# Squares of the RMS norms: VectorE adds the first five or four tiles, TensorE sums that tile and the rest

## The chip, the core and the metric

The kernel runs on one NeuronCore of a Trainium2 chip. The metric is device time in microseconds of one launch, the median over several runs. The engines meant below are TensorE (PE in the profile, PEld for its weight loads), VectorE (DVE), ScalarE (ACT), GpSimd (POOL) and SyncE (SP), whose queue starts most of the weight transfers.

## The reference, cut to what matters

A residual stream `x` of 256 tokens by 1024 features passes through ten sublayers, each of which begins with an RMS norm of `x`:

```python
def rms_norm(h, gain):
    h32 = h.astype(jnp.float32)
    h32 = h32 * lax.rsqrt(jnp.mean(h32 * h32, axis=-1, keepdims=True) + EPS)
    return (h32 * gain.astype(jnp.float32)).astype(h.dtype)

# first block, for each of 2 layers
h = rms_norm(x, norm_g[layer, 0]) * (1.0 + scale[:, :, 0]) + shift[:, :, 0]
x = x + 0.5 * gate[:, :, 0] * swiglu(h, ffn_w_in[layer, 0], ffn_w_down[layer, 0])
...   # then attention or hgrn2, whose last product is "@ w_o", then swiglu again
# second block, for each of 2 layers
x = x + sliding_window_attention(rmsnorm(x, norm_mix[i]), ...)   # or short_gated_conv
x = x + peer_ffn(rmsnorm(x, norm_ffn[i]), ...)
```

The change concerns only the sum of squares over the 1024 features, `mean(h32 * h32)`.

## The kernel before

`x` lies transposed in SBUF as `xT`: features on the 128 partitions, in KD = 8 tiles of 256 tokens. A norm needs, for each token, a sum over 8 tiles and 128 partitions. ScalarE squares a tile of `xT` into a tile of `sq` as soon as that tile has its final value, and TensorE sums over the partitions: the tile of squares is the stationary operand, a column of ones moves, and the result goes to one column of the PSUM bank `mz[:, 0]`. `sums(n, a, b)` does it for tiles a to b-1 of norm n, with two matmuls a tile (one for each half of the tokens). The sum then goes to ScalarE (square root), VectorE (reciprocal) and back to TensorE, which spreads it over the partitions (`spread_norm`).

Weights are float32 and are split in two parts. A chunk of weights lands in `raw` (four slots), ScalarE copies its high part to `w_hi` (L1534), VectorE subtracts and writes the low part `w_lo` over `raw` (L2108), and TensorE multiplies with both. `lo_ready` tells TensorE that a chunk is split; `w_used` tells SP, ScalarE and VectorE that TensorE is done with it, and a slot is filled again only then. Each engine has one hand-written order of work, and all of it waits on counting semaphores.

Two places stand ahead of a norm, four times each.

* The second feed-forward product, `ffn` with the phase `ffn_down`, ahead of norms 1, 3, 4 and 6. It has eight pairs `rp` of two chunks `j` (11 tiles of weights each). A pair makes one tile of `xT`, which VectorE adds at its end (`add_to_x`, L2211 and L2213). TensorE calls `sums` for one tile ahead of the second chunk of pairs 2 to 6 (tiles 0 to 4), and ahead of each chunk of pair 7 (tiles 5 and 6). In each pair VectorE splits two chunks, in the first three of these phases does up to two columns of the modulation (`modulation`, L2176, on `ada_raw`, which ScalarE fetches), from pair 5 on makes two tiles of the next product's input (`raw_low`, L2133), and then waits for `w_used` and adds to `xT`.
* The output projection, `out_product`, ahead of norms 2, 5, 7 and 9. It has four chunks `c`, each of which makes two tiles of `xT`. After chunk 2 TensorE sums tiles 0 and 1, after chunk 3 tiles 2 and 3. VectorE splits, calls `raw_low` for the two tiles of the chunk before, waits for `w_used` and adds to `xT`.

Behind both, `raw_pair` starts the next phase on the not yet normalized `x` (L639 to L641), sums the remaining tiles of squares between its matmuls, and begins with

```python
pe.wait_ge(evac_done, ph.evac0)
pe.wait_ge(lo_ready, 2 * pair + 2)
```

so it waits until both chunks of its first pair are split; VectorE does that during the last chunks of the phase before. Norm 0 stands at the kernel's start: there VectorE adds all eight tiles of squares (L2925). Norm 8 stands behind the experts and is not touched.

Of the kernel before, what the change touches and what calls it, by code (L numbers as in the profile page):

```python
# [30 lines left out]
AX = mybir.AxisListType  # L31
# [37 lines left out]
def raw_pairs(ph):  # L69

    return ph.pairs if ph.kind in ("swa", "query", "conv") else RAW_PAIRS

# [144 lines left out]
def build(nc, x, cols, const, pick, lvmask, rel, bucket, c_row, ada, ffn_in, ffn_down, attn, out_w, hgrn, swa, conv,  # L217
# [10 lines left out]
    with ExitStack() as ctx:  # L228
# [189 lines left out]
        norm_sq, norm_sum, norm_rms = sem("norm_sq"), sem("norm_sum"), sem("norm_rms")  # L418
        norm_inv, norm_wide = sem("norm_inv"), sem("norm_wide")
# [171 lines left out]
        def _(pe):  # L591
# [7 lines left out]
            def sums(n, a, b):  # L599

                for k in range(a, b):
                    pe.wait_ge(norm_sq, KD * n + k + 1)
                    for tb in range(TB):
                        last = mm(mz[:, 0, tb:tb + 1], sq[:, k, tb * P:(tb + 1) * P], ones[:, 0:1], start=(k == 0 and tb == 0),
                                  stop=(k == KD - 1), skip_group_check=True)
                if b == KD:
                    last.then_inc(norm_sum, 1)
# [192 lines left out]
            def ffn(q, n):  # L800
# [10 lines left out]
                for rp, pair, half, lap in each_pair(ph):  # L811
                    if rp > 1:
                        pe.wait_ge(x_done, KD * n + rp - 1)
                    for j in range(2):
# [4 lines left out]
                        if j and 1 < rp < KD - 1:  # L819
                            sums(n + 1, rp - 2, rp - 1)  # L820
                        if rp == KD - 1:
                            sums(n + 1, rp - 2 + j, rp - 1 + j)
# [463 lines left out]
            def out_product(i, n, opening=halves_first):  # L1286
# [21 lines left out]
                for rp, pair, half, lap in each_pair(ph.part(1, ph.pairs - 1)):  # L1308
                    for j in range(2):
                        c = 2 * rp + j  # L1310
                        pe.wait_ge(lo_ready, 2 * pair + j + 1)
                        pe.wait_ge(x_done, KD * n + 2 * c - 2)
                        for t in range(2):
                            last = tile_product(pp[:, j, t], 2 * half + j, t * KD, us, 0, KD, KD - 1)
                        last.then_inc(w_used, 1)
                        sums(n + 1, 2 * c - 4, 2 * c - 2)
# [783 lines left out]
        def _(dve):  # L2100
# [107 lines left out]

            def add_to_x(ps, g, xk, done):
# [5 lines left out]
            def ffn(q, n):  # L2215
# [39 lines left out]
                for rp, pair, half, lap in each_pair(ph):  # L2255
# [3 lines left out]
                    if rp > 4:  # L2259
                        for k in range(2 * rp - 10, 2 * rp - 8):  # L2260
                            raw_low(n + 1, k)
                    if rp == 7:
# [13 lines left out]
            def out_product(i, n):  # L2276
# [3 lines left out]
                for rp, pair, half, lap in each_pair(ph):  # L2280
                    for j in range(2):
# [4 lines left out]
                        if c:  # L2286
                            raw_low(n + 1, 2 * c - 2)
                            raw_low(n + 1, 2 * c - 1)
                        dve.wait_ge(w_used, 2 * pair + j + 1)
# [919 lines left out]
```

## Time and profile before

| | us |
|---|---|
| median of 3 runs | 2913.57 (2910.48 to 2914.21) |
| the profiled execution, its own time | 2913.14 |
| its span, first to last instruction | 2911.3 |
| TensorE busy with matmuls | 2801.7 (96%) |
| VectorE busy | 2300.0 (79%) |
| ScalarE busy | 1379.6 (47%) |

The busy times count instructions of an engine that overlap in time once. The profiled execution stands within 0.5 us of the median, so a time read from its rows can be compared with the runs. "Idle before" names the time in which the engine did nothing ahead of an instruction, with what ended it.

### The profile page before, as it was taken

The numbers are of one execution on the slowest core, as the hardware profiler recorded it, in microseconds if no ns is written. First come the engines' busy times: TensorE is split into PE (matmuls) and PEld (weight loads), VectorE is DVE, ScalarE is ACT, GpSimd is POOL, SyncE is SP. The second block draws the span as 40 slices with busy tenths as digits, with TensorE's granted clock in tenths as the row PEclk, the third lists the DMA queues.
The fourth block names the chain that finished last, engine by engine and source line by source line (L and its number), as shares of the span: only waits on it lengthen the run. The fifth ranks groups of instructions, "written<-read, shape, count | busy, mean of one in ns | idle before, by whom it ended". The sixth has DMA issues, their size and how long they took to land.

```text
span 2911.3 us, 48985 instructions
## 1 busy us (share of the span) xinstructions
PE 2801.7 (96%) x19360; PEld 2600.1 (89%) x19360; DVE 2300.0 (79%) x3460; ACT 1379.6 (47%) x1553; POOL 816.1 (28%) x663
## 2 busy tenths in 40 slices
PE   5999899999999999999999999999999999999999
PEld 3888788888889888789999989999999999999998
DVE  7788768888875765667959978888778959978887
ACT  4444545454444544454445554444444445545444
POOL 2310313113131120005992013321006981023221
PEclk9999999999999999999999999999999999999999
DMA  7777247777843465334457779999454557779997
GB/s 298 282 278 278 73 144 268 284 251 277 286 159 116 171 217 178 116 116 172 176 179 259 263 260 325 372 377 376 160 188 174 178 197 256 256 276 333 361 390 295
DMA packets 161902, 699.99 MB, mean 240 GB/s; under 512 B 15240, under 2 KB 61488, under 8 KB 105536
## 3 DMA queue, kind: packets, MB, share of 16 engines
q1 hardware_dynamic: 122720, 559.65, 53.2%
q10 hardware_dynamic: 20576, 70.85, 6.6%
q0 software_dynamic: 18432, 67.12, 6.3%
q8 instruction: 115, 1.88, 0.3%
q14 instruction: 59, 0.48, 0.0%
HBM read 667.07 MB, written 30.42 MB: 240 GB/s over the span
## 4 chain that ended last, share of the span: by engine, by line
PE 54%; POOL 5%; DVE 4%; DMA 2%; ACT 2%; issue 1%; ACTq 0%; SPq 0%; DVEq 0%
PE pp L1426 6%; PE mz L1426 6%; PE pp L1353 6%; PE pp L628 5%; POOL w_lo L2990 5%; PE mz L1428 3%; PE pp L1355 3%; PE pp L1428 3%; PE pp L1331 3%; PE pp L1333 3%; PE pp L1332 3%; PE pp L630 2%; PE pp L639 2%; PE pp L641 2%; PE pp L640 2%; DMA raw<-expert_v 2%
## 5 line engine op out<-in xcount | busy, mean ns | idle before, releaser
L1534 ACT ACTIVATE w_hi<-raw 128x2048 fp32r<-128x2048 f32 (+1 forms) x486 | 893.3, 1839 | 396.7 <-DMA raw<-expert_v 203.6
L2108 DVE TENSOR_TENSOR w_lo<-raw,w_hi 128x2048 fp32r<-128x2048 f32 (+1 forms) x400 | 874.1, 2186 | 240.5 <-ACT w_hi L1534 239.4
L2990 POOL TENSOR_TENSOR w_lo<-raw,w_hi 128x512 fp32r<-128x512 f32 x288 | 402.3, 1437 | 718.5 <-ACT w_hi L1534 717.6
L628 PE MATMUL pp<-hs,w_hi 128*128 128x512 f32 x1408 | 511.1, 406 | 24.2 <-POOL hs L3073 12.6
L630 PE MATMUL pp<-hs,w_lo 128*128 128x256 f32 x1408 | 398.7, 283 | 0.0
L1426 PE MATMUL mz<-w_split,w_hi 128*128 128x448 f32 x1024 | 355.0, 377 | 7.0 <-issue 7.0
L628 PEld LDWEIGHTS pp<-hs,w_hi 128*128 128x128 f32 x1408 | 269.3, 191 | 99.0 <-DVE w_lo L2108 11.5
L1426 PE MATMUL pp<-w_split,w_hi 128*128 128x448 f32 x1024 | 353.1, 376 | 2.2 <-DVE w_split L2818 1.9
L628 PE MATMUL pp<-us,w_hi 128*128 128x512 f32 x960 | 345.4, 403 | 9.0 <-DVE both L2127 4.2
L1353 PE MATMUL pp<-hs,w_hi 128*128 128x448 f32 x1024 | 328.9, 377 | 1.3 <-POOL w_lo L2990 1.3
L1331 PE MATMUL pp<-hs,w_hi 128*128 128x224 f32 x1024 | 285.0, 278 | 12.5 <-POOL w_lo L2990 12.2
L1333 PE MATMUL pp<-hs,w_lo 128*128 128x224 f32 x1024 | 283.5, 277 | 0.0
L1332 PE MATMUL pp<-hs,w_hi 128*128 128x224 f32 x1024 | 283.4, 277 | 0.0
L1428 PE MATMUL mz<-w_split,w_lo 128*128 128x224 f32 x1024 | 272.1, 266 | 0.0
L1355 PE MATMUL pp<-hs,w_lo 128*128 128x224 f32 x1024 | 271.6, 265 | 0.0
L630 PEld LDWEIGHTS pp<-hs,w_lo 128*128 128x128 f32 x1408 | 271.0, 192 | 0.0
L1428 PE MATMUL pp<-w_split,w_lo 128*128 128x224 f32 x1024 | 270.5, 264 | 0.0
L630 PE MATMUL pp<-us,w_lo 128*128 128x256 f32 x960 | 269.3, 280 | 0.0
L639 PE MATMUL pp<-xs,w_hi 128*128 128x256 f32 (+1 forms) x864 | 247.6, 287 | 6.6 <-issue 3.2
L641 PE MATMUL pp<-xs,w_lo 128*128 128x256 f32 (+1 forms) x864 | 244.2, 283 | 0.0
L640 PE MATMUL pp<-xs,w_hi 128*128 128x256 f32 x864 | 244.0, 282 | 0.0
L2978 POOL CAST us<-u 128x256 f32 (+1 forms) x88 | 95.4, 1085 | 497.9 <-DVE u L2241 269.6
(362 smaller groups left out, 5800.7 us busy)
## 6 DMA issues: line engine op xcount, KB each, us to landing
raw<-expert_u SPq DMA_DIRECT2D x128, 1024.0 KB, 4.9
raw<-expert_v SPq DMA_DIRECT2D x128, 1024.0 KB, 7.3
raw<-ffn_in SPq DMA_DIRECT2D x88, 1024.0 KB, 4.8
ada_raw<-ada ACTq DMA_DIRECT2D x116, 512.0 KB, 5.2
raw<-ffn_down SPq DMA_DIRECT2D x64, 704.0 KB, 5.3
raw<-out_w SPq DMA_DIRECT2D x16, 1024.0 KB, 4.7
raw<-hgrn SPq DMA_DIRECT2D x16, 1024.0 KB, 4.8
raw<-query SPq DMA_DIRECT2D x16, 1024.0 KB, 4.7
```

The source lines that it names most:

```text
L628: mm(outp, w_hi[:, slot, a:a + P], rhs[:, k0 + k].rearrange("p a t -> p (a t)"), start=(k0 + k == 0), stop=False, skip_group_check=True)
L630: last = mm(outp[:, 0:T], w_lo[:, slot, a:a + P], rhs[:, k0 + k, 0, :], start=False, stop=(k0 + k == last_k), skip_group_check=True)
L1331: mm(dst, wh, hs[:, k, 0, FEW:T], start=(k == 0), stop=False, skip_group_check=True)
L1332: mm(dst, wh, hs[:, k, 1, FEW:T], start=False, stop=False, skip_group_check=True)
L1333: last = mm(dst, wl, hs[:, k, 0, FEW:T], start=False, stop=(k == KD - 1), skip_group_check=True)
L1353: mm(dst[:, 0:2 * TD], w_hi[:, 2 * half + j, a:a + P], hs[:, k, :, FEW:T], start=(k == 0), stop=False, skip_group_check=True)
L1355: last = mm(dst[:, 0:TD], w_lo[:, 2 * half + j, a:a + P], hs[:, k, 0, FEW:T], start=False, stop=(k == KD - 1), skip_group_check=True)
L1426: mm(acc[:, 0:2 * TD], w_hi[:, 2 * half + j, a:a + P], w_split[:, j, e].rearrange("p a t -> p (a t)"), start=start, stop=False, skip_group ...
L1428: return mm(acc[:, 0:TD], w_lo[:, 2 * half + j, a:a + P], w_split[:, j, e, 0], start=False, stop=False, skip_group_check=True)
L1534: f(w_hi[:, slot, 0:n], raw[:, slot, 0:n], ACT.Copy).then_inc(hi_ready, 1)
L2108: v.tensor_tensor(w_lo[:, slot, 0:n], raw[:, slot, 0:n], w_hi[:, slot, 0:n].bitcast(F32), ALU.subtract)\
L2990: last = g_.tensor_tensor(w_lo[:, slot, a:a + n], raw[:, slot, a:a + n], w_hi[:, slot, a:a + n].bitcast(F32), ALU.subtract)
```

## The change

VectorE gets one new instruction in each of the eight places, `add_squares`: a `tensor_reduce` that adds the first 5 tiles of squares (behind `ffn_down`, in pair 6, between `raw_low` and the wait for `w_used`) or the first 4 (in `out_product`, at chunk 2, also between `raw_low` and the wait for `w_used`) and writes the result to `sq[:, 7]`, whose own squares come later. A new semaphore `sq_added` counts them. TensorE's `sums` skips the tiles that were added, and at the last of them takes `sq[:, 7]` instead, behind a wait for `sq_added`. The calls move: behind `ffn_down` none is left in pairs 2 to 6, and ahead of the first chunk of pair 7 one call takes the added tile and tile 5; in `out_product` one call for the added tile stands in the middle of chunk 3, between its two products, and the two calls behind chunks 2 and 3 are gone.

```diff
+def added_tiles(n):
+    return 0 if n in (0, NORMS - 2) else 5 if n in (1, 3, 4, 6) else 4
+
+def added_before(n):
+    return n - (n > NORMS - 2)
...
             def sums(n, a, b):
-                for k in range(a, b):
-                    pe.wait_ge(norm_sq, KD * n + k + 1)
+                first = max(added_tiles(n) - 1, 0)
+                for k in range(max(a, first), b):
+                    if k == first and k:
+                        pe.wait_ge(sq_added, added_before(n))
+                    else:
+                        pe.wait_ge(norm_sq, KD * n + k + 1)
                     for tb in range(TB):
-                        last = mm(mz[:, 0, tb:tb + 1], sq[:, k, tb * P:(tb + 1) * P], ones[:, 0:1], start=(k == 0 and tb == 0),
+                        src = sq[:, KD - 1 if k == first and k else k, tb * P:(tb + 1) * P]
+                        last = mm(mz[:, 0, tb:tb + 1], src, ones[:, 0:1], start=(k == first and tb == 0),
...   # TensorE, ffn_down
-                        if j and 1 < rp < KD - 1:
-                            sums(n + 1, rp - 2, rp - 1)
                         if rp == KD - 1:
-                            sums(n + 1, rp - 2 + j, rp - 1 + j)
+                            sums(n + 1, 4 + 2 * j, 6 + j)
...   # TensorE, out_product
                         for t in range(2):
+                            if c == 3 and t:
+                                sums(n + 1, 3, 4)
                             last = tile_product(pp[:, j, t], 2 * half + j, t * KD, us, 0, KD, KD - 1)
                         last.then_inc(w_used, 1)
-                        sums(n + 1, 2 * c - 4, 2 * c - 2)
...   # VectorE
+            def add_squares(n):
+                count = added_tiles(n)
+                dve.wait_ge(norm_sq, KD * n + count)
+                v.tensor_reduce(sq[:, KD - 1], sq[:, 0:count].rearrange("p k t -> p t k"), AX.X, ALU.add).then_inc(sq_added, 1)
...   # VectorE, ffn_down
+                    if rp == 6:
+                        add_squares(n + 1)
...   # VectorE, out_product
+                        if c == 2:
+                            add_squares(n + 1)
```

## Rows read from the trace of the kernel before

**Rows 1.** Groups of instructions by form, TensorE, whole span.

```profile
L604 PE MATMUL mz<-consts,sq 128*128 128x1 f32 x288 | 35.7, 237 | 4.0 <-ACT sq L1591 3.8
```

**Rows 2.** Timeline of TensorE (start, us): a call for one tile, for two.

```profile
194.48 0.28 PE L630 MATMUL pp<-us,w_lo 128*128 128x256 f32 x1
194.59 0.50 PE L604 MATMUL mz<-consts,sq 128*128 128x1 f32 x4
...
195.27 0.28 PE L630 MATMUL pp<-us,w_lo 128*128 128x256 f32 x1
...
195.62 0.28 PE L630 MATMUL pp<-us,w_lo 128*128 128x256 f32 x1
...
965.21 0.95 PE L604 MATMUL mz<-consts,sq 128*128 128x1 f32 x8
966.01 0.48 PE L628 MATMUL pp<-us,w_hi 128*128 128x512 f32 x1
```

**Rows 3.** Groups by form, VectorE, whole span: the two kinds of reduction.

```profile
L2925 DVE TENSOR_REDUCE sq_sum<-sq 128x256 f32<-128x2048 f32 x1 | 3.6, 3648 | 1.6 <-ACT sq L1591 1.6
L2324 DVE TENSOR_REDUCE small<-scores 128x2 f32<-128x512 f32 x8 | 5.5, 686 | 0.3
```

**Rows 4.** Timeline of VectorE: the first addition to tile 6 in the four ffn_down.

```profile
233.78 0.47 DVE L2211 SCALAR_TENSOR_TENSOR xT<-pp,a_gate,xT 128x256 f32<-128x256 f32 x1
...
600.39 0.47 DVE L2211 SCALAR_TENSOR_TENSOR xT<-pp,a_gate,xT 128x256 f32<-128x256 f32 x1
...
801.94 0.48 DVE L2211 SCALAR_TENSOR_TENSOR xT<-pp,a_gate,xT 128x256 f32<-128x256 f32 x1
...
1159.01 0.48 DVE L2211 SCALAR_TENSOR_TENSOR xT<-pp,a_gate,xT 128x256 f32<-128x256 f32 x1
```

**Rows 5.** Timeline of TensorE: the sum that opens pair 7, first and third ffn_down.

```profile
231.17 0.50 PE L604 MATMUL mz<-consts,sq 128*128 128x1 f32 x4
...
797.18 0.50 PE L604 MATMUL mz<-consts,sq 128*128 128x1 f32 x4
```

**Rows 6.** Timeline of TensorE: the first matmul of raw_pair behind each ffn_down.

```profile
240.78 0.35 PE L639 MATMUL pp<-xs,w_hi 128*128 128x258 f32 x1
...
609.03 0.36 PE L639 MATMUL pp<-xs,w_hi 128*128 128x258 f32 x1 [1.28 <-issue]
...
809.46 0.28 PE L639 MATMUL pp<-xs,w_hi 128*128 128x258 f32 x1
...
1169.39 0.36 PE L639 MATMUL pp<-xs,w_hi 128*128 128x256 f32 x1 [1.91 <-issue]
```

**Rows 7.** Groups by line, VectorE, windows 218:234 and 1143:1159.5: splits and their idle.

```profile
L2108 DVE TENSOR_TENSOR w_lo<-raw,w_hi 128x1408 fp32r<-128x1408 f32 x4 | 6.5, 1623 | 1.5 <-ACT w_hi L1534 1.5
...
L2108 DVE TENSOR_TENSOR w_lo<-raw,w_hi 128x1408 fp32r<-128x1408 f32 x4 | 6.5, 1626 | 5.8 <-ACT w_hi L1534 5.7
```

**Rows 8.** Timelines, second output projection: VectorE at chunks 2 and 3, then raw_pair.

```profile
967.90 0.48 DVE L2211 SCALAR_TENSOR_TENSOR xT<-pp,a_gate,xT 128x256 f32<-128x256 f32 x1
...
969.72 2.28 DVE L2108 TENSOR_TENSOR w_lo<-raw,w_hi 128x2048 fp32r<-128x2048 f32 x1
...
972.46 0.37 PE L639 MATMUL pp<-xs,w_hi 128*128 128x258 f32 x1
```

**Rows 9.** The same, first and third output projection: chunk 3's split, then raw_pair.

```profile
405.78 2.28 DVE L2108 TENSOR_TENSOR w_lo<-raw,w_hi 128x2048 fp32r<-128x2048 f32 x1
...
410.07 0.36 PE L639 MATMUL pp<-xs,w_hi 128*128 128x258 f32 x1
...
1281.65 2.28 DVE L2108 TENSOR_TENSOR w_lo<-raw,w_hi 128x2048 fp32r<-128x2048 f32 x1
...
1284.72 0.37 PE L639 MATMUL pp<-xs,w_hi 128*128 128x256 f32 x1
```

**Rows 10.** TensorE after an idle; a window: us, busy times (x), granted clock, DMA.

```profile
803.53 0.35 PE L604 MATMUL mz<-consts,sq 128*128 128x1 f32 x2 [1.93 <-ACT sq L1591]
...
805.45:808.80 3.35, 3.35 (x13) 2.87 (x12) 2.75 (x3) 2.45 (x4) 0.00 (x0) 0.50 0.13 54
```

More of the change, by code:

```diff
@@ L418, in build @@
         norm_sq, norm_sum, norm_rms = sem("norm_sq"), sem("norm_sum"), sem("norm_rms")
+        sq_added = sem("sq_added")
         norm_inv, norm_wide = sem("norm_inv"), sem("norm_wide")
```

## The prediction

> **What bounds the kernel now.** I read the page first, and in it the shares of the engines in the table above: TensorE is busy for 2801.7 of 2911.3 us. The reader is to see that a matmul taken out of its queue is worth its time, unless another engine is what it waits for next. Then I read the groups by form: the sums of squares are 288 records of 128x1, two for each matmul, 35.7 us in all for nine norms [rows 1]. That is the pool from which the change takes. Last came the timelines of TensorE and VectorE side by side at the eight places. There the reader is to see something that the shares hide. VectorE is busy 79% overall, but at the end of the second feed-forward products it is behind TensorE: in the first of them TensorE begins pair 7 at 231.17 [rows 5], which means that pair 6 is done, and VectorE adds pair 6's tile only at 233.78 [rows 4], with no idle time ahead of it. It was splitting, taking modulation columns and calling raw_low until then. In the third it is 797.18 against 801.94. So VectorE has no free time just where the change gives it more to do.
>
> **What is removed from TensorE.** A call for one tile stretches the distance between two L630 from the usual 0.35 us (195.27 to 195.62) to 0.79 (194.48 to 195.27), so it costs 0.44 us [rows 2]. A call for two tiles costs 0.80 us (965.21 to 966.01). Behind an ffn_down seven one-tile calls, 3.1 us, become one of two tiles and one of one, 1.24 us; up to pair 7 it is 2.2 us less (the five calls of pairs 2 to 6). In an output projection two calls of two tiles, 1.60 us, become one of 0.44. In all 4 x 1.84 + 4 x 1.16 = 12.0 us of TensorE's queue. If nothing else waited, that would be the gain.
>
> **What is added to VectorE.** No row has a reduction of this very size. The nearest is norm 0's, the same layout with 8 tiles: 3.648 us for 2048 elements [rows 3], 1.78 ns an element, so 2.28 us for 5 tiles and 1.82 us for 4. The bound below is the dense reduction, 0.686 us for 512, or 1.34 ns an element with its fixed part: 1.6 us for 5 tiles at two such rows and a half (1.72), 1.37 for 4. The bound above takes what norm 0's row has over four dense ones (3.648 - 4 x 0.686 = 0.90 us) as a price of the 256 outputs, which does not shrink with the tiles: 1.72 + 0.90 = 2.6 and 1.37 + 0.90 = 2.3 us. I take the middle, since the access pattern is that of norm 0.
>
> On this the Trainium skill has two rules. "VectorE: DVE Perf Modes", in "Rules for kernel authors", says that a tensor_reduce on the hot path runs at the lowest rate and should be restructured away, which speaks against this change; its table gives 2293 ns for 2048 fp32 elements at that rate, by which an estimate for 5 tiles is 1.4 us. "SBUF — State Buffer", in the section on the DMA port swizzle, says that accesses which leave a 16-byte line each time pay a penalty, which would put it above that. The row of 3.648 us lies on the side of the second; by the first the sum below would be some 5 us smaller.
>
> **Behind ffn_down: where the stall arises.** TensorE now waits for sq_added at the start of pair 7. VectorE does the addition in pair 6, behind two splits, two modulation columns and two raw_low, so at the place in its order where L2211 stood in the trace. Call that time D. Queued behind the waiting TensorE is all of pair 7 and with it the next phase; queued behind VectorE's reduction is the addition to tile 6, and behind it ScalarE's square of tile 6 and its next split. The first matmul of raw_pair then stands at D + 2.28 (reduction) + 0.14 (from the end of the instruction waited for to the sum, as at 803.53 [rows 10]) + 0.80 (two tiles) + 3.80 (a chunk, 11 tiles at 0.345 [rows 2]) + 0.44 + 3.80 = D + 11.3.
>
> D can move forward only by what VectorE idles for weights, since a faster TensorE frees slots earlier: 1.5 us in the first (218 to 234) [rows 7], and as much in the second, whose window looks the same (the first stands for both). In the third its only idle is 0.6 for ada_raw, which TensorE does not speed up: 0. In the fourth, which has no modulation, it idles 5.8 us in the last pairs [rows 7], so it follows TensorE by the four calls that lie ahead of the slot it waits for: 1.76. With D from [rows 4] and the old starts from [rows 6]:
>
> first: 233.78 - 1.5 + 11.3 = 243.6 against 240.78, +2.8; second: 600.39 - 1.5 + 11.3 = 610.2 against 609.03, +1.2; third: 801.94 + 11.3 = 813.2 against 809.46, +3.8; fourth: 1159.01 - 1.76 + 11.3 = 1168.6 against 1169.39, -0.8. In the second and fourth the old start was itself a wait for the split of raw_pair's weights, 1.28 and 1.91 us, and the new stall swallows that. Sum: +7.0 us.
>
> **In the output projections.** The reduction starts where VectorE began chunk 2's addition, 967.90 in the second, and ends at 969.7; TensorE reaches the middle of chunk 3 at 965.21 + 2.8 = 968.0, so it stands there for 1.8 us [rows 2, 8]. What decides is what comes after: chunk 3's split, which raw_pair needs, slips by 1.82. Its start plus 1.82 + 2.28 + 0.12 gives the new raw_pair: 969.72 becomes 973.9 against 972.46, +1.5 [rows 8]; 405.78 becomes 410.0 against 410.07, -0.1; 1281.65 becomes 1285.9 against 1284.72, +1.1 [rows 9]. The fourth repeats the third, +1.1. Sum: +3.6 us. Here VectorE goes from one piece of work to the next without idling, so a faster TensorE brings nothing forward. The additions to xT of chunk 3 also come later, by 1 to 2 us, under raw_pair's first 6 us of matmuls, and cost nothing.
>
> **The clock.** After the idle of 1.93 us at 803.53 the stretch 805.45 to 808.80 has a granted clock of 0.50, the 1.2 GHz level, in which work of 1.7 us takes 3.35 [rows 10]. The new idles at pair 7 are longer: 231.17 - 2.2 = 229.0 until 234.7 in the first, 5.7 us, about 6 in the second, 9 in the third, 3 in the fourth. I put 2 us on each, between one such stretch (1.7) and somewhat more, and take off the 1.7 that the fourth pays in the old trace, just behind its idle of 1.91 us: 2 + 2 + 2 + 0.3 = +6.3 us. The third's 1.7 is not taken off, because the old start of 809.46 already holds it and D + 11.3 doesn't. The bound below is 0 (an idle need not be followed by a drop), the bound above twice this.
>
> **The sum.** 7.0 + 3.6 + 6.3 = 16.9 us. What follows each place is work that hangs on TensorE's progress, so the shifts add up. On the profiled execution's own time, 2913.14 (2911.3 of span and 1.8 around it), that is 2930.0. The median of the runs is 2913.57, 0.4 higher, which changes nothing at this size: 2930.
>
> **Rivals.**
> (A) The cover holds: VectorE runs ahead by more than I think once its idles are gone, and TensorE never waits for sq_added. Then the 12.0 us are a gain: 2901.6. It needs D plus the reduction to lie ahead of pair 7's start, so VectorE some 5 to 9 us earlier than in [rows 4, 5], with 1.5 us of idle to gain from. Against it speaks every ffn_down but the fourth. Half of it, only the output projections and the fourth ffn_down gaining, would give about 2910.
> (B) The stall comes, but the clock stays up and the reduction is cheap. With 1.72 and 1.37 us the sums become 7.0 - 4 x 0.56 = 4.8 and 3.6 - 4 x 0.45 = 1.8, and the clock 0: +6.6, 2920.
> (C) The stall is dearer: reductions at 2.6 and 2.3 (+1.3 and +1.9), nothing of D moved forward (+4.8), clock drops twice as long (+6): 2944.
> (D) The delays are paid back: while TensorE stands, transfers and splits run ahead, and the raw pairs behind, which wait here and there for a split, lose those waits. With (B)'s prices that leaves about 2915, no change that can be told.
>
> **How the numbers follow.** Changes under 0.2% (5.8 us) can hardly be told from none. My forecast, between 2924 and 2938, has a chance of 0.50; (B) 0.15; (C) 0.15; (D) 0.10, (A) with its half 0.10. Faster by over 0.2% is most of (A): 0.07. Within 0.2%: (D) and the half of (A), with little else: 0.12. Slower: 0.81. The range runs from between (D) and (B), 2916, to (C), 2944; the likeliest case's own is 2924 to 2938.
>
> **What the profile of the changed kernel would show.** Right: TensorE idle of 3 to 9 us ahead of the first sum of pair 7, ended by VectorE's reduction; idle of 1 to 2 us in the middle of chunk 3 in three output projections; L604 down from 288 records to 176; reductions of about 2.3 and 1.8 us; granted clock 0.50 behind the long idles. Wrong: no idle ahead of the sums, or the start of raw_pair closer to that of pair 2 than before in the first three ffn_down. The weakest step is D: if VectorE gets there earlier than its idle allows, most of the loss goes.

## The result, and the profile after

| | before | changed |
|---|---|---|
| median of 4 runs, us | 2912.03 (2905.29 to 2914.21) | 2945.53 (2939.91 to 2951.02) |
| ratio, 95% interval | | 1.0112 [1.0083, 1.0141] |
| profiled execution, us | 2913.14 | 2944.71 |
| its span, us, and mean granted clock | 2911.3, 0.987 | 2942.5, 0.98 |

The kernel became slower by 1.1%, 32.6 us by the ratio. The forecast was slower by 16.9 us, 2930, with a range up to 2944: the direction came, the size is about twice as large, and the median of 2945.53 stands above the range.

In the profile after, the first rows are the page's busy times; then come two groups by form, TensorE's sums and VectorE's reductions (count | busy, mean ns | idle before).

```profile
PE 2801.2 (95%) x19248; PEld 2594.8 (88%) x19248; DVE 2341.1 (80%) x3468; ACT 1379.8 (47%) x1553; POOL 806.6 (27%) x663
...
L620 PE MATMUL mz<-consts,sq 128*128 128x1 f32 x176 | 24.4, 255 | 32.4 <-DVE sq L2228 32.4
...
L2228 DVE TENSOR_REDUCE sq<-sq 128x256 f32<-128x1280 f32 x4 | 9.3, 2322 | 0.0
L2228 DVE TENSOR_REDUCE sq<-sq 128x256 f32<-128x1024 f32 x4 | 7.8, 1948 | 0.0
```

The sums' idle time is the result in one number: 4.0 us ahead of L604 before [rows 1] have become 32.4 us ahead of L620, all of it ended by VectorE's reduction. 112 records went, and TensorE is busy hardly less than before (2801.7), because what runs behind the idles runs at the lower clock and counts longer.

The timeline of TensorE shows the eight places. First the sums that open pair 7 in the four ffn_down, with the idle in brackets, and behind them the first matmul of raw_pair, which answers to [rows 6].

```profile
239.64 0.34 PE L620 MATMUL mz<-consts,sq 128*128 128x1 f32 x1 [9.83 <-DVE sq L2228]
...
252.34 0.28 PE L655 MATMUL pp<-xs,w_hi 128*128 128x258 f32 x1
...
612.42 0.34 PE L620 MATMUL mz<-consts,sq 128*128 128x1 f32 x1 [6.95 <-DVE sq L2228]
...
624.78 0.28 PE L655 MATMUL pp<-xs,w_hi 128*128 128x258 f32 x1
...
818.93 0.34 PE L620 MATMUL mz<-consts,sq 128*128 128x1 f32 x1 [9.85 <-DVE sq L2228]
...
830.62 0.29 PE L655 MATMUL pp<-xs,w_hi 128*128 128x258 f32 x1
...
1181.54 0.24 PE L620 MATMUL mz<-consts,sq 128*128 128x1 f32 x1 [2.59 <-DVE sq L2228]
...
1192.16 0.28 PE L655 MATMUL pp<-xs,w_hi 128*128 128x256 f32 x1
```

From the sum to raw_pair I counted 0.80 + 3.80 + 0.44 + 3.80 = 8.84 us. Here they are 12.70, 12.36, 11.69 and 10.62. The windows from the first sum to the end of pair 7 say why. Columns: us, busy times (x), then the granted clock, the DMA share and GB/s.

```profile
239.64:252.30 12.66, 12.66 (x56) 11.23 (x57) 6.41 (x7) 4.11 (x5) 0.00 (x0) 0.69 0.21 78
612.42:624.70 12.28, 12.28 (x56) 10.90 (x57) 6.41 (x7) 4.10 (x5) 0.00 (x0) 0.71 0.24 85
818.93:830.60 11.67, 11.67 (x56) 10.34 (x57) 6.41 (x7) 4.10 (x5) 0.00 (x0) 0.77 0.26 88
1181.54:1192.10 10.56, 10.56 (x56) 9.33 (x57) 6.41 (x7) 4.42 (x6) 0.00 (x0) 0.84 0.43 165
```

TensorE is busy all the time in them, at a mean granted clock of 0.69 to 0.84. The stretches mix the two levels, 1.2 and 2.4 GHz, and in this trace the shortest idle has the highest mean behind it. The part on the clock below shows that other traces don't keep to that order.

The timeline of VectorE ahead of the first of these sums shows the reduction and what it stood behind; the addition to tile 6, L2232, answers to [rows 4].

```profile
235.06 1.23 DVE L2191 SCALAR_TENSOR_TENSOR ada_raw<-ada_raw,c_all 128x1024 f32<-128x1024 f32 x1 [2.52 <-DMA ada_raw<-ada]
...
237.19 2.30 DVE L2228 TENSOR_REDUCE sq<-sq 128x256 f32<-128x1280 f32 x1
239.41 0.47 DVE L2232 SCALAR_TENSOR_TENSOR xT<-pp,a_gate,xT 128x256 f32<-128x256 f32 x1
```

The reader is to see that VectorE had not even begun the reduction when TensorE had already stood for 7.4 of its 9.8 us. Of the four phases from the first matmul of an ffn_down to the first of raw_pair, the lengths in the two traces are these:

| ffn_down | before, us | after, us | longer by | forecast, clock included |
|---|---|---|---|---|
| first | 66.0 | 77.3 | 11.3 | 4.8 |
| second | 67.8 | 73.0 | 5.2 | 3.2 |
| third | 69.1 | 76.8 | 7.7 | 5.8 |
| fourth | 66.7 | 66.9 | 0.2 | -0.5 |

The output projections' raw_pair starts are the last rows; the starts of before are in [rows 8, 9]. The first sum in the second projection is shown with its idle, and so is that of the third; the first's idle is 0.21 us and the fourth's 1.39.

```profile
418.81 0.36 PE L655 MATMUL pp<-xs,w_hi 128*128 128x258 f32 x1 [0.53 <-issue]
...
991.02 0.61 PE L620 MATMUL mz<-consts,sq 128*128 128x1 f32 x4 [0.21 <-DVE sq L2228]
...
995.09 0.36 PE L655 MATMUL pp<-xs,w_hi 128*128 128x258 f32 x1 [0.57 <-issue]
...
1304.04 0.27 PE L620 MATMUL mz<-consts,sq 128*128 128x1 f32 x1 [1.39 <-DVE sq L2228]
...
1308.78 0.41 PE L655 MATMUL pp<-xs,w_hi 128*128 128x256 f32 x1
```

The trace after is already late by 8.80, 21.09 and 22.25 us where these three projections begin, and by 8.74, 22.63 and 24.06 at their raw_pair: they add -0.1, +1.5 and +1.8. The fourth adds +1.0 (30.70 to 31.75).

### The profile page after: what moved, and what is told of

Its sections match the earlier page's. It is cut to its first block, busy times and chain, and to the rows that moved or that the text cites. A ratio compares the mean times of both kernels' runs of the same rounds, so it can differ in the third digit from the quotient of the medians.

```text
span 2942.5 us, 48750 instructions
## 1 busy us (share of the span) xinstructions
PE 2801.2 (95%) x19248; PEld 2594.8 (88%) x19248; DVE 2341.1 (80%) x3468; ACT 1379.8 (47%) x1553; POOL 806.6 (27%) x663
## 4 chain that ended last, share of the span: by engine, by line
PE 48%; DVE 10%; DMA 3%; POOL 3%; ACT 2%; issue 1%; ACTq 0%; SPq 0%; DVEq 0%
PE pp L1368 6%; PE pp L1441 6%; PE mz L1441 6%; PE pp L644 4%; PE pp L1370 3%; PE pp L1443 3%; PE mz L1443 3%; POOL w_lo L3015 3%; PE pp L655 2%; DMA raw<-expert_v 2%; PE pp L657 2%; PE pp L656 2%; PE pp L646 2%; ACT w_hi L1549 1%; PE mz L1430 1%; DVE w_lo L2123 1%
## 5 line engine op out<-in xcount | busy, mean ns | idle before, releaser
L3015 POOL TENSOR_TENSOR w_lo<-raw,w_hi 128x512 fp32r<-128x512 f32 x288 | 395.5, 1411 | 732.2 <-ACT w_hi L1549 731.6
L644 PE MATMUL pp<-hs,w_hi 128*128 128x512 f32 x1408 | 510.6, 405 | 23.4 <-POOL hs L3098 12.9
L644 PE MATMUL pp<-us,w_hi 128*128 128x512 f32 x960 | 351.9, 409 | 9.3 <-DVE both L2142 4.2
L644 PEld LDWEIGHTS pp<-hs,w_hi 128*128 128x128 f32 x1408 | 268.3, 191 | 98.3 <-DVE w_lo L2123 10.4
L644 PEld LDWEIGHTS pp<-us,w_hi 128*128 128x128 f32 x960 | 186.5, 194 | 55.0 <-issue 5.5
```

Of the source, the lines that this page charges most:

```text
L644: mm(outp, w_hi[:, slot, a:a + P], rhs[:, k0 + k].rearrange("p a t -> p (a t)"), start=(k0 + k == 0), stop=False, skip_group_check=True)
L3015: last = g_.tensor_tensor(w_lo[:, slot, a:a + n], raw[:, slot, a:a + n], w_hi[:, slot, a:a + n].bitcast(F32), ALU.subtract)
```

## The experiments

Each ratio is to runs of the kernel before on the same chip in the same session, and a difference given behind a ratio follows from the ratio; where the medians say something else, both stand. Two more traces of each unchanged kernel show how much traces differ by themselves. Idles and phases come from one profiled execution of each kernel, which can lie up to 13 us from its median.

**Which places cost.** Only the ffn_down part is kept:

```diff
-    return 0 if n in (0, NORMS - 2) else 5 if n in (1, 3, 4, 6) else 4
+    return 5 if n in (1, 3, 4, 6) else 0
...   # out_product: the calls of the kernel before, no add_squares
```

> Only the four norms behind the second feed-forward products are changed; the output projections keep the code of before. Theory S (TensorE stands at the new wait for VectorE's sum at the start of pair 7, where VectorE is already late): the changed kernel's trace has those idles at 9.8, 7.0, 9.9 and 2.6 us, so nearly the whole loss is here: 22 to 28 us over before. Rival W (the loss is spread, half of it made in the output projections and in the first expert stage, where the traces also differ by 6 us): 10 to 16 us.

Measured: 2941.11 us against 2915.33, ratio 1.0089 [1.0065, 1.0113], about 26 us, inside theory S's 22 to 28. Idles ahead of pair 7's sums: 6.77, 5.78, 5.81, 2.78 us, in a profiled execution of 2929.42, the shortest of the four.

Only the output projections are kept (added_tiles gives 4 for norms 2, 5, 7 and 9, else 0; ffn_down as before):

> Only the four norms behind output projections are changed. Theory S: VectorE's addition of 1.9 us delays chunk 3's split, which the next phase waits for, and the idle at the new wait is 0.2 to 1.4 us: 2 to 5 us over before, the forecast was 3.6. Rival W: 10 us or more.

Measured: 2920.75, ratio 1.0021 [1.0004, 1.0039], 6 us. So four fifths of the loss lie behind ffn_down, and the two parts together (31 us) are the whole change. The forecast of +3.6 for the output projections lies in the interval (1 to 11 us).

**Is it the place of the wait?** In ffn_down the first call moves from ahead of pair 7's first chunk to ahead of its second, a chunk (3.8 us) later:

```diff
-                        if rp == KD - 1:
-                            sums(n + 1, 4 + 2 * j, 6 + j)
+                        if rp == KD - 1 and j:
+                            sums(n + 1, 4, 7)
```

> As the changed kernel, but behind the feed-forward products TensorE takes the added tile and tile 5 ahead of the last chunk of pair 7, with tile 6, and not ahead of the first. Theory S (what costs is where the wait stands): TensorE does a chunk, 3.8 us, before it waits, so each idle gets up to 3.8 us shorter and the fourth goes: 13 to 18 us less than the changed kernel, 14 to 20 us over before. Rival V (what costs is VectorE's extra time, which delays the addition to tile 6, its square and the next splits, wherever TensorE waits): within 5 us of the changed kernel, 27 us or more over before.

Measured: 2937.71, ratio 1.0062 [1.0033, 1.0090]. The first wait in its timeline:

```profile
237.53 0.34 PE L620 MATMUL mz<-consts,sq 128*128 128x1 f32 x1 [3.10 <-DVE sq L2228]
```

The idles are 3.10, 2.89, 1.89 and 0, and the four phases sum to 272.0 us, where three traces of the changed kernel have 294.0, 290.6 and 287.9 and three of the kernel before 269.6, 266.3 and 272.1. Most of the stall is gone. By the ratios 15 us are, 1.0112 against 1.0062, but the two intervals just overlap, and by its median this kernel still stands 22 us over before. Its trace says where: the first matmul of raw_pair behind the third projection stands at 1288.22, only 5.7 us behind the mean of three traces of before (1282.5), where the changed kernel's three are 23.3 us behind. The rest comes later, where only the fourth projection is changed (about 1 us).

**Is it the reduction?** No reduction and no wait for it; TensorE sums only the later tiles, so that the first four or three are left out of the sum:

```diff
-                    if k == first and k:
-                        pe.wait_ge(sq_added, added_before(n))
...
+                    pe.wait_ge(norm_sq, KD * n + k + 1)
...   # and no add_squares
```

> As the changed kernel without VectorE's additions and the wait for them: TensorE takes tile 4 (or 3) itself, the tiles of squares before it are left out of the sum. It shows what the 56 matmuls alone are worth. Theory M (they lie on the path nearly everywhere): 8 to 12 us under before. Rival N (other waits eat it, since VectorE and the transfers set the pace at the ends of these phases): 0 to 4 us under before.

Measured: 2909.11, ratio 0.9979 [0.9962, 0.9995], 6 us faster where TensorE has 12.0 us less to do, between the two forecasts. In its first ffn_down, window 232:240, the sum waits again, now for ScalarE's square, which waits for VectorE's addition to x:

```profile
PE mz L617 <- ACT sq L1603: 4.8, 1, 4.8
```

So even a free addition gives back only about half. The first phase lasts 73.7 us in this trace, more than in any trace of before; VectorE's waits for modulation columns in it sum to 9.9 us. The profiled execution, 2922.56, is the slowest of the ten.

**Another engine adds.** GpSimd adds the tiles one by one into a buffer of its own (`sq_sum`), and VectorE does nothing:

```diff
+            def add_squares(n):   # GpSimd
+                count = added_tiles(n)
+                for k in range(1, count):
+                    pool.wait_ge(norm_sq, KD * n + k + 1)
+                    last = g_.tensor_tensor(sq_sum[:], sq[:, 0] if k == 1 else sq_sum[:], sq[:, k], ALU.add)
...
+                last.then_inc(sq_added, 1)
```

> As the changed kernel, but GpSimd, which has nothing to do there, adds the tiles of squares one by one as they come, into a tile of their own; VectorE gets nothing. Theory S/V (all of the loss is VectorE's part, in its time or in its being waited for): no idle at the new wait, and the time falls to what the version without additions gave, 3 to 12 us under before. Rival P (GpSimd's additions slow VectorE's or come late themselves): at before or above.

Measured: 2920.89 against 2913.21, ratio 1.0027 [1.0011, 1.0043], 8 us slower, on the side of rival P and not the 3 to 12 us of gain that theory S/V asked for. No stall at pair 7 ends with the addition. At pair 7 of the second and third ffn_down the timeline has, instead:

```profile
593.34 0.24 PE L621 MATMUL mz<-consts,sq_sum 128*128 128x1 f32 x1 [1.54 <-issue]
...
794.20 0.24 PE L621 MATMUL mz<-consts,sq_sum 128*128 128x1 f32 x1 [2.14 <-issue]
```

"issue" here is time for which the profile shows no releaser; VectorE's split of the coming weights ends just before, which I take for the wait. The phases sum to 266.7 us, at the lower end of before's (266.3 to 272.1), with 7.4 us less in TensorE's queue. I read this as work time that TensorE is given and can't use, since VectorE's splits pace these phases; the rows don't prove it. What makes this kernel 14 us dearer than no_add stays open. It does not show up to the third projection: its raw_pair starts at 1278.11, 4.4 us ahead of the mean of before.

**Are the late modulation columns the cause?** VectorE waits for transfers of these ahead of pair 7, in the trace after more than before. Two kernels transfer only 64 of 1024 entries of each in ffn_down (the rest is stale, so the modulation is not the reference's), on top of the change and of the kernel before:

```diff
-                act.dma_start(ada_raw[:, j, 0:per], src).then_inc(ada_in[j], 16)
+                w = 64 if ph.kind == "ffn_down" else D
+                act.dma_start(ada_raw[:, j, 0:per, 0:w], src[:, :, 0:w]).then_inc(ada_in[j], 16)
```

> As the changed kernel, but in the second feed-forward products each transfer of a modulation column brings 64 of its 1024 entries a row; VectorE still reads all 1024, the rest is old. Its work is the same, only the wait for the transfer goes. Theory T (the prediction's D failed because VectorE waited longer for ada_raw than in the trace of before, 6.2 us in the first such phase against 2.4): the idles at pair 7 become 5 to 6, 5 to 6, 5 to 8 and 2.6 us as forecast, and the distance to the next kernel, which has the same short transfers and the code of before, is 12 to 18 us. Rival U (the waits for ada_raw play no part): idles of 9 to 10 us stay in the first and the third.

> The kernel before with the same short transfers of modulation columns, as the base for the run ahead. Theory T: 0 to 6 us under before, since in the third feed-forward product TensorE waited 1.9 us for a late square behind a VectorE that idled on ada_raw. Rival U: as before.

Measured: the changed kernel 2937.56, ratio 1.0078 [1.0055, 1.0101]; the kernel before 2907.88, ratio 0.9981 [0.9957, 1.0005]. The distance between them, 1.0%, is nearly that between the whole kernels. The first idle in the changed one:

```profile
234.33 0.24 PE L620 MATMUL mz<-consts,sq 128*128 128x1 f32 x1 [4.33 <-DVE sq L2229]
```

The idles are 4.33, 4.17, 3.94 and 2.63, some 14 us less than in the trace after, but the four phases are 280.4 us against 261.5, 18.9 more. Theory T was right that the waits for transfers lengthen the idles, and wrong on the distance: 12 to 18 us forecast, about 28 by the two ratios. The loss is there without these waits, so they are not its cause.

This pair also splits the loss. The reduction starts 55.8, 56.4, 56.1 and 54.8 us behind the start of its phase, in all 5.3 us earlier than the addition to tile 6 in before_short_load, where the prediction moved it forward by 4.8. With D + 11.3 the phases would be some 7 us longer than in before_short_load, as forecast (7.0). The other 12 us arise between the reduction and raw_pair: from the sum to raw_pair it takes 10.66, 12.21, 12.21 and 12.26 us instead of 8.84.

**The clock by itself.** TensorE does matmuls that nobody reads while it would stand (18, 12, 18 and 4 calls of `keep_warm` in the four ffn_down):

```diff
+                            if j == 0:
+                                keep_warm(mz[:, 2], (18, 12, 18, 4)[q])
```

> As the changed kernel, but TensorE does 18, 12, 18 and 4 matmuls without use (256 columns, into a free bank) ahead of its wait at the start of pair 7, so that it doesn't idle there. Theory C (the idle costs twice: the wait itself, and a lower granted clock behind it, 1.8 to 3.9 us in each of the four places in the changed kernel's trace): no stretch of clock 0.50 in pair 7 and 6 to 12 us under the changed kernel. Rival: the clock has no part in the loss, within 3 us of the changed kernel or over it.

Measured: 2934.32 against 2913.99, ratio 1.0058 [1.0042, 1.0074]. The timeline at the first place, and the window behind it:

```profile
228.03 7.93 PE L608 MATMUL mz<-consts 128*128 128x256 f32 x36
...
237.14 0.27 PE L620 MATMUL mz<-consts,sq 128*128 128x1 f32 x1 [1.19 <-DVE sq L2230]
...
246.29 0.28 PE L655 MATMUL pp<-xs,w_hi 128*128 128x258 f32 x1
...
237.00:249.00 12.00, 11.86 (x79) 10.89 (x80) 8.10 (x11) 5.58 (x8) 0.00 (x0) 1.00 0.36 117
```

With the idles filled the granted clock is 1.00 in pair 7 at all four places, and from the sum to raw_pair TensorE takes 9.14, 9.15, 9.11 and 9.14 us. (In the third place the 18 calls ran on past the reduction's end and held the sum up by 1.4 us.) In the trace after it took 12.70 + 12.36 + 11.69 + 10.62, 12.0 us over 4 x 8.84. So 10.8 us of these are the clock's, and 1.2 come from my count of 8.84, which is 0.3 too short at each place. The time lies 8 us under the unchanged copy in the same session (2942.10, below), and by the two ratios 16 us, where theory C had 6 to 12. The clock was a true part of the loss, and larger than the 8 us that I had put on the four idles.

**How late is VectorE without the length of the reduction?** It reduces one tile only (four or three are left out of the sum), 0.41 us:

```diff
-                v.tensor_reduce(sq[:, KD - 1], sq[:, 0:count].rearrange("p k t -> p t k"), AX.X, ALU.add).then_inc(sq_added, 1)
+                v.tensor_reduce(sq[:, KD - 1], sq[:, 0:1].rearrange("p k t -> p t k"), AX.X, ALU.add).then_inc(sq_added, 1)
```

> As the changed kernel, but VectorE's addition reads one tile of squares in place of 5 or 4 (the other tiles are left out of the sum): same place, same waits, less work, some 0.5 us in place of 2.34 and 1.9. Theory L (VectorE is already 3 to 5 us late there, the reduction comes on top): each stall gets shorter by the 1.4 to 1.9 us alone, in all 8 to 14 us under the changed kernel, still 15 us or more over before. Rival R (the reduction is what stalls TensorE): the stalls at pair 7 go altogether, 3 us over before or less.

Measured: 2926.70, ratio 1.0029 [1.0006, 1.0051]. The idles stay:

```profile
235.27 0.34 PE L620 MATMUL mz<-consts,sq 128*128 128x1 f32 x1 [7.95 <-DVE sq L2228]
```

They are 7.95, 9.71, 3.79 and 0.99. The eight reductions are 14 us shorter (4 x 1.91 + 4 x 1.54), and the time is 15 us under the copy's 2942.10, or 24 by the two ratios. So half of the loss or more goes with the reductions' length, and 8 us (by the ratio) to 13 us (by the medians) over before stay with an addition of hardly any length, because TensorE must wait at a place that VectorE reaches late. That lies between L, which asked for 15 us or more, and R. The trace doesn't show the split: its four phases sum to 289.5 us, no less than the changed kernel's, since VectorE waited 8.2 us for modulation columns in the second alone (idle 9.71), and the stretch from the sum to raw_pair is as long as with full reductions, 12.48, 12.63, 12.21 and 10.72.

**The addition behind the additions to x.** In ffn_down the reduction goes behind tile 6's addition (so that ScalarE's square is not held up), and TensorE takes its result as late as can be, in raw_pair just ahead of tile 7:

```diff
-                    if rp == 6:
-                        add_squares(n + 1)
...   # behind add_to_x of the same pair:
+                    if rp == 6:
+                        add_squares(n + 1)
...   # TensorE: tiles 5 and 6 at pair 7; in raw_pair
+                    if count == 5 and k == KD - 1:
+                        tiles = ["added", k]
```

> As the changed kernel, but behind the feed-forward products VectorE adds the squares after it has added to tile 6, into a tile of their own, and TensorE takes that tile in raw_pair just ahead of tile 7's, so nothing of pair 7 hangs on it. Theory S (place of the wait): the stalls of 7 to 10 us at pair 7 go, what is left is the old wait for tile 6's square and 2.3 us of VectorE ahead of the next weights: 0 to 8 us over before, most of it from the output projections. Rival V (VectorE's time is the cost, wherever it stands): 15 us over before or more.

Measured: 2920.84, ratio 1.0022 [1.0003, 1.0041], the same as with the output projections alone. The phases sum to 268.1 us, within before's three. The first wait at pair 7 is now for the square of tile 6, as in the kernel before:

```profile
236.40 0.24 PE L627 MATMUL mz<-consts,sq 128*128 128x1 f32 x1 [3.45 <-ACT sq L1613]
```

With the addition and the wait in these places the part behind ffn_down costs nothing, and gains nothing either, though TensorE has less to do. Here both have moved; sum_later moved the wait alone, by one chunk, and kept part of the loss.

**Without transfers and without reductions.** no_add and the short transfers together (the same parts left out):

> The version without additions (the 56 matmuls gone, no wait for VectorE, the first tiles left out of the sum) together with the short transfers of modulation columns. Theory M (the matmuls are worth their 12 us, but only where VectorE is not late; with the full transfers it was, so that version gained 6): now it stands 8 to 12 us under the kernel before with the same short transfers, whose ratio to before was 0.9981, so about 0.9945. Rival N (VectorE's own work, not the transfers, holds TensorE in these phases): 3 to 6 us under it, 0.9965.

Measured: 2906.84 against 2914.65, ratio 0.9965 [0.9946, 0.9984]. Phases 253.7 us, 7.8 under before_short_load's 261.5, where I count 4 x 1.84 = 7.4 for the matmuls. In this pair of traces the removed matmuls are worth their time in ffn_down, where VectorE is early. In the timed runs of the two kernels it is not to be told: the intervals overlap, and the ratio is the one that rival N named.

**The same kernels again.** Unchanged copies, one run and one trace each, to learn how much a trace differs from the next:

> The kernel before, unchanged, for a second trace of it. If what differs in the first expert stage (6 us made good until 1500 us, 12 us lost until 1600) and at the start of the first feed-forward product (up to 3 us) belongs to the state of the transfers and not to the change, it shows here too: offsets between the two traces of before of several us that no code explains. If not, the two traces stay within 1 us of each other throughout.

> The changed kernel once more, for a second trace. If VectorE's single instruction of 27.5 us in the first expert stage is chance, it may be missing here, and then the trace ends some 6 us sooner against its own start of that stage; the idles at pair 7 should again be near 10, 7, 10 and 2.6 us, with the first and third moving with the waits for ada_raw.

> The kernel before a third time, trace only. The waits for ada_raw were 2.4, 0 and 8.1 us and then 0.4, 0 and 0.1. If they are chance, a sum like the changed kernel's can show; if the change draws them out, they sum to under 8 us again. A VectorE instruction of 20 to 30 us in an expert stage has shown in none of the two traces; one here says that it has nothing to do with the change.

> The changed kernel a third time, trace only. The waits for ada_raw in the first three feed-forward products were 6.2, 1.6 and 5.5 us and then 6.7, 2.7 and 1.0. If a faster TensorE draws them out, they sum to 8 us or more here; if they are chance, they may be as low as in the second trace of before, 0.5 us. A VectorE instruction of 20 to 30 us in an expert stage: about one chance in three.

Measured: before 2917.18 and 2924.29, changed 2942.10 and 2943.84. Means of three profiled executions: 2918.2 and 2943.6, 25.4 us apart. Mean lengths of the four phases: 67.4, 67.3, 68.6, 66.0 before, 77.0, 73.6, 72.9, 67.3 changed: +9.6, +6.3, +4.4, +1.3, in all +21.5 where the forecast had 13.3. At the raw_pair behind the third projection the means are 1282.5 and 1305.8, 23.3 us apart, where the forecast had 15.8. Summed over the first three phases, VectorE's waits for modulation columns are 10.5, 0.5 and 10.4 us in before's three traces and 16.7, 12.9 and 7.9 in the changed kernel's, so they overlap. A long VectorE instruction in an expert stage came in the third trace of before too.

The kernels here that are faster than the kernel before leave part of the computation out.

## Why the prediction was right in direction and too small

**Right.** The place and the mechanism of the stall: TensorE stands at the first sum of pair 7 for VectorE's reduction, behind which pair 7 and the next phase are queued. L620 has 176 records. The reductions take 2.32 and 1.95 us, where I took 2.28 and 1.82; "VectorE: DVE Perf Modes" of the Trainium skill (section "Rules for kernel authors") was right that a tensor_reduce should not stand on the hot path, but its table's rate, by which I estimated 1.4 us for 5 tiles, is not what this access pattern runs at. The raw_pair starts of the projections moved by -0.1, +1.5, +1.8 and +1.0, against -0.1, +1.5, +1.1 and +1.1. The forecast ahead of raw_pair, D + 11.3, closes in the first ffn_down once the 3.8 us more that the sum-to-raw_pair stretch took there are put in: 237.19 + 11.3 + 3.8 = 252.3, as the row has it. In kept_warm, where the clock stays up, raw_pair starts 11.5, 11.6 and 11.6 us behind the reduction's start in the first, second and fourth.

**The first step that failed: D, the time at which VectorE comes to tile 6.** I moved it forward by 1.5, 1.5, 0 and 1.76 us, by what VectorE idled for weights. In the trace after it is 237.19 in the first instead of 232.3, 4.9 us later than forecast. VectorE stood there for modulation columns: in window 170:240 of the two traces, grouped by line, the idle ahead of them grew.

```profile
L2176 DVE SCALAR_TENSOR_TENSOR ada_raw<-ada_raw,c_all 128x1024 f32<-128x1024 f32 x16 | 19.5, 1220 | 2.4 <-DMA ada_raw<-ada 2.4
```

```profile
L2191 DVE SCALAR_TENSOR_TENSOR ada_raw<-ada_raw,c_all 128x1024 f32<-128x1024 f32 x16 | 19.5, 1221 | 6.2 <-DMA ada_raw<-ada 6.2
```

The other three reductions start here:

```profile
609.93 2.34 DVE L2228 TENSOR_REDUCE sq<-sq 128x256 f32<-128x1280 f32 x1
...
816.48 2.30 DVE L2228 TENSOR_REDUCE sq<-sq 128x256 f32<-128x1280 f32 x1
...
1179.05 2.35 DVE L2228 TENSOR_REDUCE sq<-sq 128x256 f32<-128x1280 f32 x1
```

Relative to the beginning of its phase, D is later than forecast by 4.6 us in the first, 0.5 in the second and 1.1 in the third, and 0.8 earlier in the fourth. In all 5.3 us. I had counted one kind of VectorE's waits as cover, and forgotten that the other kind could change. It can also shrink: the prediction's 0.6 us for the third was the wait in its last pairs, and the whole phase had 8.1 us of them in the trace of before (window 745:805) and 0.1 in the second trace of it. In the later two traces of the changed kernel D comes 4.7 us earlier in the third than forecast, and over the four places it is off by 4.6 and 0.1 us in all. So this step failed by what one trace of before happened to hold. Whether the change itself draws the waits out is not settled. Where they are away, in short_load, D moved as forecast, and the loss was there all the same.

**The second step, and the one that failed in every trace: the clock.** I put 2 us on each of four idles and took 1.7 off for the fourth, 6.3 in all. Measured, over 8.84 us: 3.9, 3.5, 2.9 and 1.8, in all 12.0. kept_warm shows that 10.8 of these are the clock's, and that the chunks and sums themselves were counted 0.3 too short at each place. The 1.7 us that I took off lie behind the fourth's raw_pair start and can't be found in its phase. I had read the price off one idle of 1.93 us, and bounded it by twice that. Nor does the price follow the idle's length: from the sum to raw_pair it takes 11.68 us behind an idle of 10.03 (second trace of the changed kernel), 12.21 behind one of 4.17 (short_load) and 10.72 behind one of 0.99 (fourth place of small_add), against 9.1 with the clock up. Over the three traces of the changed kernel D was 3.3 us off in the mean, and the stretch behind it 11.1 us over the count instead of 6.3.

**The bookkeeping of the two main traces.** Forecast up to 1284.72 (the stage ahead of the experts): 15.8 us. To this come 5.3 for D, 5.7 for the clock and the short count (12.0 against 6.3), and 0.8 for the projections: 27.6. Outside the phases 3.5 us net were paid back (the delay is 11.56 us behind the first ffn_down and 8.80 at the first projection's start, grows from 8.74 to 10.54 and falls from 15.75 to 13.48 ahead of the second and third, and small ones). That leaves 24.1; the trace has 24.06.

**What was not the change.** Of the trace's 31.1 us at the end, 6.6 more arise between 1284.72 and the last projection, in the first expert stage, where the change does nothing. From the third projection's raw_pair to the fourth projection the two traces have 843.7 and 837.1 us; the seventeen traces have 837.1 to 854.1, so before's is the shortest of all and the changed kernel's an ordinary one. One VectorE instruction lasts 27.5 us there and in the trace of before 1.25; the last section tells of it. This is chance, and a part of why this pair of traces is 31.6 us apart, where the means of three are 25.4. The later changed runs lie 28 and 29 us over their sessions' medians of before (2913.99 and 2914.65), so a few of the 32.6 us by the ratio are not placed by any trace.

**The parts of the prediction on side effects.** "Idle of 1 to 2 us in the middle of chunk 3 in three output projections" held in two, the third and fourth (1.39 each); in the second it was 0.2, as in the first. In the second the half clock took its place. Behind a wait of 1.95 us for an addition to x, which both traces have at this place, TensorE's matmuls of chunk 2 go at 0.63 us instead of 0.40:

```profile
980.99 0.40 PE L644 MATMUL pp<-us,w_hi 128*128 128x512 f32 x1
...
981.91 0.63 PE L644 MATMUL pp<-us,w_hi 128*128 128x512 f32 x1
...
983.83 0.63 PE L644 MATMUL pp<-us,w_hi 128*128 128x512 f32 x1
...
984.98 0.40 PE L644 MATMUL pp<-us,w_hi 128*128 128x512 f32 x1
```

In the trace of before the granted clock is 1.00 behind the same wait (window 958:966). TensorE comes some 1.7 us later to the sum and hardly waits; the start of raw_pair is set by VectorE's split all the same.

**The rivals.** (A), that the cover holds, fell at all four ffn_down. (B), cheap reductions and a clock that stays up, fell too. So did (D): of some 27.6 us only 3.5 were paid back. (C) was the nearest in size, 2944, but not in its reasons: the reductions were nearly as forecast, D and the clock were dearer. Its bound of "nothing moved forward" was no bound, since D can also move back.

## What to carry to other kernels

Work moved off an engine that is busy 96% pays only if the receiver is ahead at that very place, so set the two timelines side by side there, and count all of the receiver's waits, those for transfers too. If it is behind, the wait for its result can cost several times the work saved. Here the same addition cost 26 us behind ffn_down with the wait at the start of pair 7, against 7.4 us of matmuls saved, and nothing with the addition behind the additions to x and the wait in raw_pair. Price an idle of a busy TensorE twice, by itself and by the clock behind it, and take the second price from more than one idle: here it was 1.5 to 3.6 us behind idles of 1 to 10 us, and didn't follow their length. And take several traces of the kernel before: a single pair held 6 us of chance.

## What the runs showed of the hardware that was not expected

In an expert stage one VectorE instruction can last 18 to 31 us while GpSimd does one split after the other. The timelines of the changed kernel's first expert stage, VectorE and GpSimd, show it; then come the same for the third trace of the kernel before, and last the instruction of the same form in the first trace of the kernel before, with GpSimd's row there. The first row of GpSimd is cut off by its window at either end.

```profile
1501.44 27.51 DVE L2715 CAST top_b<-top_i 128x256 bf16<-128x256 uint32 x1
...
1489.00 41.10 POOL L3015 TENSOR_TENSOR w_lo<-raw,w_hi 128x512 fp32r<-128x512 f32 x32
```

```profile
1459.78 30.96 DVE L2684 TENSOR_TENSOR cand<-top_v 128x1024 f32<-128x1024 f32 x1
...
1443.57 57.08 POOL L2990 TENSOR_TENSOR w_lo<-raw,w_hi 128x512 fp32r<-128x512 f32 x44 [2.52 <-ACT w_hi L1534]
```

```profile
1448.94 57.01 POOL L2990 TENSOR_TENSOR w_lo<-raw,w_hi 128x512 fp32r<-128x512 f32 x39 [2.54 <-ACT w_hi L1534]
...
1474.87 1.25 DVE L2690 CAST top_b<-top_i 128x256 bf16<-128x256 uint32 x1
```

The 32 splits of GpSimd in 41.1 us are 1.3 us each, so VectorE stood over some 21 of them. Such an instruction of 18 to 31 us is in seven of the seventeen traces, of either kernel and of experiments. Six of them have it in the first expert stage; from the third projection's raw_pair to the fourth projection they take 843.7 to 854.1 us, in the mean 848.3, and the other eleven 837.1 to 847.6, in the mean 842.6. GpSimd's splits run on behind it. In the first trace of before GpSimd has such a row without a gap as well, and VectorE isn't held up, so a row of splits is not enough to bring it about; six of its some 40 splits take 2.3 or 3.3 us instead of 1.3, where the changed kernel's row from 1479 on has one such in 43. "SBUF — State Buffer" of the Trainium skill, in "SBUF: two separate sides", has VectorE and GpSimd share a port pair, locked for one whole instruction while the other blocks, where the VectorE instruction runs in a two-port mode or has two inputs in SBUF. That VectorE is held up while GpSimd works agrees with the rows; that it lasts over some 21 instructions on end is not told there. I did not test this cause by an experiment; it is argued from the rows alone.
